# Order of the gated embedding, the output projection and the query projection in a one-core transformer block kernel

## The chip, the cores and the metric

The kernel runs on one core of one Trainium2 chip. Its time is the device time of one execution in microseconds (us); several executions give a median. One further execution was recorded by the hardware profiler; all rows below come from that one.

Engine names: PE is TensorE (matmul), with PEld for its weight loads, DVE is VectorE, ACT is ScalarE, POOL is GpSimd, SP is SyncE, which here issues most of the DMA transfers.

## The reference, cut to what matters

The block works on 256 tokens (S) of 2048 columns (D), in float32. The part around the change is:

```
merged = gate0 * (yp @ w_branch_pool) + gate1 * (ya @ w_branch_attn)
y      = merged @ w_out                      # 2048 x 2048
x      = layer_norm(ALPHA * x + y, ln1_g, ln1_b)
q      = x @ peer_wq                         # query projection, 2048 x 2048
s1, s2 = q's halves against two tables of 128 keys -> top 16 -> 16 picks and gates per head
f      = sum over picks of gelu(x @ u[id]) * gate * v[id]      # 16384 experts
e      = sigmoid(x @ ple_gate_w) * (p @ ple_w)                 # gated embedding
x      = layer_norm(ALPHA * x + f + e, ln2_g, ln2_b)
```

The kernel computes x @ u for all experts, so the tables `u` and `v` are streamed whole, as other weights are.

## The kernel before, in words

**Weights as units.** All weights are cut into units of 128 x 1024 float32 (512 KB). A unit goes through a ring: SP loads it into one of four RAW slots; ACT copies it to one of four HI slots with the high part of each number; DVE makes LO = RAW - HI in one of two slots (line 765); PE multiplies with HI and then with LO. Each product is thus three products: activations high with HI, activations low with HI, activations high with LO. In the order of each engine's program ACT's conversion (`conv`, line 453) runs three units ahead of PE (`ACT_LEAD`), DVE's one unit ahead (`DVE_LEAD`). SP may load a slot again when DVE has made LO of its last content (`lo_ready`); ACT may write HI of unit u when PE has done unit u-4; DVE may write LO of unit u when PE has done unit u-2 (`unit_done`). Everything an engine does is one queue in program order; semaphores are the only links between the engines.

**Two shapes of unit.** `w_unit` keeps weights stationary and streams activations: 8 matmuls of 128x512 (line 1350) and 8 of 128x256 (line 1356). `n_unit` keeps activations stationary and streams the weights: 8 matmuls of 128x512 with HI (line 1370) and 4 with LO (line 1377). Its results fill all eight PSUM banks: for each of two token tiles, four quarters of 512 columns (`nbank(tt, q)`); an even unit writes quarters 0 and 1, an odd one quarters 2 and 3.

**The phases in order** (units): ..., branch 32, wout 32, plew 4, wq 32, pleg 32, u 256, vtab 256. `branch` makes the two branch outputs, which DVE multiplies with their gates and adds in GT (lines 993, 994, 997). `wout` is the output projection. Its activations, the merged blocks, are staged two at a time: ACT copies the high part (line 610) when PE has done the units that read the slot, DVE makes the low part (line 1006), one block for two units. `plew` is p @ ple_w, from the same two slots.

**The first norm.** DVE adds y to ALPHA*x in eight pieces of 128x512 (line 1022) as the last wout unit of each column half is done, takes statistics (line 778), centres whole rows (line 784), waits for ACT's square root (line 475, with a load of its table), makes five small steps (lines 770 to 774), and rescales (line 790). ACT copies the plew result from PSUM to PW (line 624, eight pieces), PE then transposes x in 32 pieces into all eight banks (line 1392, `turn`), ACT takes the high part (line 481) and DVE the low part (line 812).

**After it.** `wq` runs with `w_unit`; ACT and DVE take each block of q out of PSUM (lines 641 and 848), PE multiplies it with the keys (line 1548) into bank 4, ACT takes the scores (line 632). After wq PE waits for the last scores to be taken and runs `pleg` (x @ ple_gate_w) with `n_unit` over all eight banks. ACT then applies the sigmoid in eight pieces (line 658), and the first `u` unit waits for the first four of them. In `u` DVE also does the top-k of one score set in each round of eight units. In the second half of u PE also makes one-hot products (line 1608), whose results DVE multiplies into the expert buffer (`spread`, line 1209); `vtab` is again `n_unit`, with stationary blocks that ACT (line 723) and DVE (line 1269) stage from the expert buffer.

**The end of u.** DVE's order after the last conversion is: `halves` (line 848, needs ACT's copy at line 710 of the last u result), `spread` (line 1209), `gated` (line 1202, needs ACT's gelu at line 713), then the low part of vtab's first block (line 1269).

## Time and profile before

| | us |
|---|---|
| median of 3 runs | 2329.09 (2329.08 to 2331.0) |
| the profiled execution | 2324.55 |
| its span, first to last instruction | 2322.9 |
| PE busy in the span | 2251.4 (97%) |
| DVE, ACT, POOL busy | 66%, 46%, 2% of the span |
| mean granted TensorE clock | 0.993 |

The DMA queues move 425 MB, 183 GB/s on average. In a timeline row the columns are start in us, duration in us, engine, source line, operation, output and inputs, shape and count of instructions merged in the row; in square brackets the idle time of that engine just before it and the instruction that ended the idle time. Matmuls overlap, and the end of a group of matmuls is modelled, so the last one's duration reaches past the start of the next group. PEclk in a windows row is the granted TensorE clock as a share of 2.4 GHz; 0.50 is 1.2 GHz.

### The profile page before, as it was taken

What the parts mean: (1) busy time and instruction counts of PE and PEld (TensorE: products, weight loads), DVE (VectorE), ACT (ScalarE), POOL (GpSimd) and SP (SyncE); (2) the same over time, 40 slices, a digit from 0 to 9 for tenths busy, and PEclk for the clock granted to TensorE, in tenths of its full rate; (3) what the DMA queues carried; (4) which work ended last, traced back from release to release, by engine and by line L of the source; (5) the groups of instructions that cost most, each with busy time, mean ns of one, the idle gap of its engine ahead of it and who ended that gap; (6) DMA issues with size and microseconds to landing.
All of it is one profiled execution on the core that took longest, in us unless ns stands there. A gap on an engine that the chain in (4) does not pass through costs nothing.

```text
span 2322.9 us, 39704 instructions
## 1 busy us (share of the span) xinstructions
PE 2251.4 (97%) x12176; PEld 1946.1 (84%) x12176; DVE 1534.6 (66%) x2806; ACT 1069.4 (46%) x1494; POOL 43.7 (2%) x89
## 2 busy tenths in 40 slices
PE   6999999899899999999999999999999999999996
PEld 5888888898688888888888888888888888888885
DVE  6547666665744479998888888887555555555556
ACT  3444555544444454445554444444444444444442
POOL 1000000000000000001000000000000000000000
PEclk9999999999999999999999999999999999999998
DMA  7555555455455656565555554545666666666663
GB/s 246 187 181 176 183 179 177 158 180 190 164 179 173 195 175 204 181 208 190 188 168 163 161 163 160 162 161 159 191 194 197 202 204 200 204 206 200 202 194 119
DMA packets 115714, 425.31 MB, mean 183 GB/s; under 512 B 13352, under 2 KB 13368, under 8 KB 114528
## 3 DMA queue, kind: packets, MB, share of 16 engines
q1 hardware_dynamic: 112608, 412.14, 55.8%
q0 software_dynamic: 3072, 12.72, 1.7%
q8 instruction: 20, 0.33, 0.1%
q14 instruction: 14, 0.11, 0.0%
HBM read 420.60 MB, written 6.31 MB: 184 GB/s over the span
## 4 chain that ended last, share of the span: by engine, by line
PE 87%; DVE 7%; issue 3%; DMA 2%; ACT 1%; DVEq 0%; SPq 0%; ACTq 0%
PE ps L1350 27%; PE ps L1370 25%; PE ps L1356 14%; PE ps L1377 12%; PE ps L1608 2%; DVE w_lo L765 2%; PE ps L1334 1%; PE ps L1338 1%; PE ps L1333 1%; DMA ln_gb<-in_ln_in 1%; DMA raw<-in_w_in 1%; DMA raw<-in_u 0%; DVE bn L778 0%; PE ps L1392 0%; PE ps L1478 0%
## 5 line engine op out<-in xcount | busy, mean ns | idle before, releaser
L765 DVE TENSOR_TENSOR w_lo<-raw,w_hi 128x1024 fp32r<-128x1024 f32 x774 | 946.5, 1223 | 491.1 <-PE ps L1377 420.5
L453 ACT ACTIVATE w_hi<-raw 128x1024 fp32r<-128x1024 f32 x774 | 821.2, 1061 | 972.8 <-DMA raw<-in_peer_v 375.9
L1350 PE MATMUL ps<-x_t_hi_lo,w_hi 128*128 128x512 f32 x3328 | 848.7, 397 | 4.6 <-ACT ple_gate L658 2.0
L1350 PEld LDWEIGHTS ps<-x_t_hi_lo,w_hi 128*128 128x128 f32 x3328 | 597.6, 189 | 114.6 <-issue 5.7
L1370 PE MATMUL ps<-w_hi,x_t_hi_lo 128*128 128x512 f32 x2592 | 643.4, 391 | 9.6 <-issue 3.2
L1370 PEld LDWEIGHTS ps<-w_hi,x_t_hi_lo 128*128 128x128 f32 x2592 | 488.0, 188 | 112.0 <-issue 6.5
L1356 PEld LDWEIGHTS ps<-x_t_hi_lo,w_lo 128*128 128x128 f32 x3328 | 452.8, 190 | 38.7 <-DVE w_lo L765 5.5
L1356 PE MATMUL ps<-x_t_hi_lo,w_lo 128*128 128x256 f32 x3328 | 464.7, 283 | 1.5 <-DVE w_lo L765 1.2
L1377 PE MATMUL ps<-w_lo,x_t_hi_lo 128*128 128x512 f32 x1296 | 347.4, 390 | 0.0
L1377 PEld LDWEIGHTS ps<-w_lo,x_t_hi_lo 128*128 128x128 f32 x1296 | 244.1, 188 | 50.7
L1189 DVE TENSOR_SCALAR onehots<-iota,i_t,gate_t 128x128 f32<-128x128 bf16 x256 | 77.8, 352 | 0.0
L1608 PE MATMUL ps<-onehots 128*128 128x128 f32 x512 | 77.1, 275 | 0.0
L1608 PEld LDWEIGHTS ps<-onehots 128*128 128x128 f32 x512 | 68.0, 192 | 0.0
L1185 DVE TENSOR_TENSOR onehots<-i_t,iota 128x256 f32<-128x256 bf16 x128 | 54.0, 422 | 19.0 <-DVE experts L1209 14.9
L1269 DVE TENSOR_TENSOR x_t_hi_lo<-experts,x_t_hi_lo 128x256 fp32r<-128x256 f32 x128 | 53.5, 419 | 0.1
L723 ACT ACTIVATE x_t_hi_lo<-experts 128x256 fp32r (+1 forms) x128 | 51.0, 400 | 0.1
L848 DVE TENSOR_TENSOR hidden<-ps,hidden 128x256 f32<-128x256 f32 x64 | 27.2, 425 | 29.3 <-ACT hidden L710 29.3
L848 DVE TENSOR_TENSOR gates_t<-ps,gates_t 128x256 f32 (+1 forms) x32 | 13.5, 423 | 45.8 <-ACT gates_t L513 45.8
L713 ACT ACTIVATE hidden<-hidden 128x256 f32<-128x256 f32 x64 | 26.8, 419 | 36.6 <-DVE hidden L848 36.6
L1209 DVE TENSOR_TENSOR experts<-ps,experts 128x512 f32 (+1 forms) x64 | 43.6, 681 | 0.0
L710 ACT ACTIVATE hidden<-ps 128x256 f32<-128x256 f32 x64 | 24.5, 383 | 38.0 <-PE ps L1356 35.7
L848 DVE TENSOR_TENSOR experts<-ps,experts 128x256 f32 x64 | 27.2, 425 | 16.3 <-ACT experts L668 10.1
(202 smaller groups left out, 1013.4 us busy)
## 6 DMA issues: line engine op xcount, KB each, us to landing
raw<-in_u SPq DMA_DIRECT2D x256, 512.0 KB, 4.4
raw<-in_peer_v SPq DMA_DIRECT2D x256, 512.0 KB, 4.7
raw<-in_w_in SPq DMA_DIRECT2D x128, 512.0 KB, 4.2
raw<-in_branch SPq DMA_DIRECT2D x32, 512.0 KB, 4.0
raw<-in_wout SPq DMA_DIRECT2D x32, 512.0 KB, 3.7
raw<-in_wq SPq DMA_DIRECT2D x32, 512.0 KB, 3.8
raw<-in_pleg SPq DMA_DIRECT2D x32, 512.0 KB, 3.8
x<-in_x SPq DMA_DIRECT2D x2, 1024.0 KB, 6.4
```

What stands on the lines that cost most here:

```text
L453: nc.scalar.activation(HI[:, u % 4, :], RAW[:, u % 4, :], ACT.Copy).then_inc(hi_ready, 1)
L723: nc.scalar.activation(XH[:, c % 4, :], BUF[:, bass.ds(val(i, 4, c), 1), :].rearrange("p a t -> p (a t)"), ACT.Copy).then_inc(ah_ready, 1)
L765: v.tensor_tensor(LO[:, u % 2, :], RAW[:, u % 4, :], HI[:, u % 4, :].bitcast(F32), ALU.subtract) \
L848: v.tensor_tensor(dst, PS[:, bank, S:2 * S], dst, ALU.add).then_inc(joined, 1)
L1185: ch.tag(v.tensor_tensor(OH[:, n % 2, :, 0, :], both.unsqueeze(2).to_broadcast([P, 2, P]), IOTA[:, :].unsqueeze(1).to_broadcast([P, 2, P]) ...
L1189: ins = v.tensor_scalar(OH[:, n % 2, r, 1, :], IOTA[:, :], I2T[:, bass.ds(t, 1)], GATET[:, bass.ds(t, 1)], ALU.is_equal, ALU.mult)
L1269: v.tensor_tensor(XL[:, c % 4, :], BUF[:, bass.ds(val(i, 4, c), 1), :].rearrange("p a t -> p (a t)"), XH[:, c % 4, :].bitcast(F32), ALU.su ...
L1350: mm(PS[:, bank, :], w(HI, u % 4)[:, k, :], XHL[:, 8 * half + k, :, :].rearrange("p a t -> p (a t)"), start=(half == 0 and k == 0), stop=F ...
L1356: r = mm(PS[:, bank, 0:S], w(LO, u % 2)[:, k, :], XH[:, 8 * half + k, :], start=False, stop=(half == 1 and k == 7))
L1370: mm(nbank(tt, 2 * half + q), stn[:, tt * P:(tt + 1) * P], HI[:, u % 4, q * 512:(q + 1) * 512], start=(first and s == 0), stop=False, skip ...
L1377: r = mm(nbank(tt, 2 * half + q), ah[:, tt * P:(tt + 1) * P], LO[:, u % 2, q * 512:(q + 1) * 512], start=False, stop=last, skip_group_chec ...
L1608: r = mm(PS[:, 4 + g % 2, o:o + P], OH[:, n % 2, t, 0, :], OH[:, n % 2, t, 1, :], start=True, stop=True)
```

## The change

1. The phase `plew` leaves the ring of units. Its four weight units are loaded by POOL's DMA queue into a buffer of their own (PRAW), spaced by wout units, and converted during wout into buffers of their own (PH, PL). p is split into high and low parts (YAH, YAL) early in wout.
2. The merged blocks are split into high and low parts for all 16 blocks (XH, XL) during `branch`, two blocks at the end of each round, and not staged in wout.
3. `wout` runs by column halves: 16 units for the left half, then 16 for the right. The residual adds and the statistics of the left half are done by DVE during the right half.
4. `pleg` moves from behind wq to ahead of it and also runs by column halves. The plew products run right after wout, the last part of them split by quarters. The norm is centred and rescaled by quarters of 512 columns, and PE transposes two column blocks at a time, between the units of the first half of pleg, into banks 2, 6, 3, 7. The sigmoids of the left half are done during the right half.
5. The square-root table is loaded ahead of wout. u follows wq at once; the last key scores are made after the first u unit, and each top-k round waits for its own scores.
6. At the end of u DVE does `spread`, then the low part of vtab's first block, then `halves` and `gated`; ACT takes that block's high part ahead of its last copy and gelu. PE's first vtab units wait for `joined`, not for `gated`.

```diff
-          ("plew", 2), ("wq", 16), ("pleg", 16), ("u", 128), ("vtab", 128)]
+          ("pleg", 16), ("wq", 16), ("u", 128), ("vtab", 128)]
...
+            pool.wait_ge(merged_ready, KD)
+            for j in range(4):
+                pool.wait_ge(unit_done, BASE["wout"] + 1 + 3 * j)
+                pool.dma_start(PRAW[:, j, :], a["plew"][j % 2, :, (j // 2) * UNIT:(j // 2 + 1) * UNIT]
+                               ).then_inc(plew_in, 16)
             pool.wait_ge(al_ready, KD)
             pool.wait_ge(ah_ready, KD)
             for n in range(2):
+                pool.wait_ge(unit_done, BASE["wout"] + 16 + 5 * n)
                 pool.dma_start(LNG[:, n, :], ...
...
+            def merged_hi(i):                                   # ACT
+                for c in range(2):
+                    act.wait_ge(merged_ready, i * 2 + c + 1)
+                    nc.scalar.activation(XH block 2i+c, GT block 2i+c, ACT.Copy).then_inc(ah_ready, 1)
+            run("branch", 8, 4, {3: merged_hi}, pre=sig_pre)
+            nc.scalar.preload_act_table(ACT.Sqrt)
+            for j in range(20):
+                conv(None, 4, BASE["wout"] + j + ACT_LEAD)
...
+                if j >= 16:
+                    act.wait_ge(plew_in, 64)
+                    nc.scalar.activation(PH[:, j - 16, :], PRAW[:, j - 16, :], ACT.Copy).then_inc(plew_hi, 1)
+            run("wout", 8, 4, {}, start=5)
             std_of(2)
+            ple_out(1, (0, 1))
+            conv(None, 4, pb + 3)
+            ple_out(2, (2,))
+            xt_hi(1, (0,))
+            ple_out(3, (3,))
+            for g in range(1, 8):
+                xt_hi(1, (g,))
+                conv(None, 4, pb + 2 * g + 2)
+                conv(None, 4, pb + 2 * g + 3)
...
+            for j in range(28):                                 # DVE
+                conv(None, 4, BASE["wout"] + j + DVE_LEAD)
...
+                if 16 <= j < 20:
+                    dve.wait_ge(plew_hi, j - 16 + 1)
+                    v.tensor_tensor(PL[:, j - 16, :], PRAW[:, j - 16, :], PH[:, j - 16, :], ALU.subtract)
+                if 20 <= j < 24:
+                    added(*first_cols[j - 20])
+                if j >= 24:
+                    quarter(X0, *first_cols[j - 24])
+            run("wout", 8, 4, {}, start=7)
+            dve.wait_ge(unit_done, BASE["wout"] + 32)
+            for tt, q in last_cols:
+                added(tt, q)
+            for tt in range(NT):
+                stats(X0, tt, (2, 3))
+            variance()
+            root(2)
+            centre_cols(X0, LNG, cols[0])
+            rescale_cols(X0, LNG, cols[0])
+            centre_cols(X0, LNG, cols[1])
+            xt_lo(1, (0,))
+            rescale_cols(X0, LNG, cols[1])
+            conv(None, 4, pb + 1)
+            for g in range(1, 8):
+                if g < 3:
+                    centre_cols(X0, LNG, cols[g + 1])
+                xt_lo(1, (g,))
+                conv(None, 4, pb + 2 * g)
+                if g < 3:
+                    rescale_cols(X0, LNG, cols[g + 1])
+                conv(None, 4, pb + 2 * g + 1)
...
+            for half in range(2):                               # PE
+                for k in range(KD):
+                    if half == 0:
+                        pe.wait_ge(al_ready, k + 1)
+                    n_unit(None, 4, BASE["wout"] + KD * half + k, XH[:, k, :], XL[:, k, :], ..., half)
+            pe.wait_ge(n_dve, 4)
+            plew_part(0, 0)
+            plew_part(0, 1).then_inc(plew_done, 1)
+            pe.wait_ge(n_dve, 8)
+            plew_part(1, 0, (0,))
+            plew_part(1, 1, (0,)).then_inc(plew_done, 1)
+            plew_part(1, 0, (1,))
+            pe.wait_ge(n_act, 6)
+            turn(1, (0,))
+            plew_part(1, 1, (1,)).then_inc(plew_done, 1)
+            for half in range(2):
+                for k in range(KD):
+                    if half == 0 and k % 2 == 0:
+                        pe.wait_ge(xh_ready, 8 + k // 2 + 1)
+                        pe.wait_ge(xl_ready, 8 + k // 2 + 1)
+                    n_unit(None, 4, BASE["pleg"] + KD * half + k, XH[:, k, :], XL[:, k, :], ..., half)
+                    if half == 0 and k % 2 == 0 and k < KD - 2:
...
+                        turn(1, (g,))
...
-            pe.wait_ge(joined, 80)
-            pe.wait_ge(peer_sb, 8)
-            for c in range(KD):
-                for j in range(2):
-                    n_unit(None, 4, BASE["pleg"] + 2 * c + j, XH[:, c, :], XL[:, c, :], c == 0, c == KD - 1)
...
-                        pe.wait_ge(n_act, 12 if j == 0 else 16)
...
+            a_lo(None, 0)                                       # DVE, end of u
+            halves(None, 2 * B_ITERS - 1)
             gated(None, 2 * B_ITERS - 1)
-            a_lo(None, 0)
             a_lo(None, 1)
...
-            pe.wait_ge(dve_evac, 79)
+            pe.wait_ge(joined, 80 + NK - 1)
```

## Rows read from the trace of the kernel before

**Rows 1.** The page: busy time by engine.
```profile
PE 2251.4 (97%) x12176; PEld 1946.1 (84%) x12176; DVE 1534.6 (66%) x2806; ACT 1069.4 (46%) x1494; POOL 43.7 (2%) x89
```

**Rows 2.** Waits of PE, 405 to 920 us: waiter, releaser, us, times, longest.
```profile
PE ps L1392 <- DVE x L790: 5.3, 2, 4.6
...
PE ps L1370 <- DVE x_t_hi_lo L1006: 2.0, 1, 2.0
...
PE ps L1548 <- DVE peer_q L848: 0.9, 1, 0.9
```

**Rows 3.** Windows, 30 wout units: busy PE, PEld, DVE, ACT, POOL; clock; DMA share, GB/s.
```profile
521.20:602.80 81.60, 81.60 (x361) 67.62 (x360) 43.14 (x45) 36.47 (x45) 1.06 (x2) 1.00 0.61 195
```

**Rows 4.** Timeline from branch to wout.
```profile
518.36 2.08 PE L1370 MATMUL ps<-w_hi,x_t_hi_lo 128*128 128x512 f32 x8 [2.49 <-issue]
```

**Rows 5.** Timeline from the last wout unit to the first wq unit.
```profile
604.62 1.07 PE L1377 MATMUL ps<-w_lo,x_t_hi_lo 128*128 128x512 f32 x4
604.74 4.87 DVE L1022 SCALAR_TENSOR_TENSOR x<-x,ps 128x512 f32<-128x512 f32 x8
607.27 2.11 PE L1370 MATMUL ps<-w_hi,x_t_hi_lo 128*128 128x512 f32 x8 [1.59 <-DVE x L1022]
...
614.93 2.47 DVE L778 BATCH_NORM_STATS2 bn<-x 128x6 f32<-128x512 f32 x4
...
618.94 4.61 DVE L784 SCALAR_TENSOR_TENSOR x<-x,mean_var,ln_gb 128x2048 f32<-128x2048 f32 x2
...
622.45 4.03 ACT L624 ACTIVATE p_w<-ps 128x512 f32<-128x512 f32 x8 [0.17 <-PE ps L1377]
...
624.60 0.16 DVE L770 RECIPROCAL rstd<-std 128x2 f32<-128x2 f32 x1
...
625.59 4.87 DVE L790 SCALAR_TENSOR_TENSOR x<-x,rstd,ln_gb 128x1024 f32<-128x1024 f32 x4
...
628.12 6.11 PE L1392 MATMUL ps<-ident,x 128*128 128x128 f32 x31 [0.66 <-DVE x L790]
...
631.12 4.88 DVE L812 TENSOR_TENSOR x_t_hi_lo<-ps,x_t_hi_lo 128x512 fp32r<-128x512 f32 x8 [0.66 <-ACT x_t_hi_lo L481]
...
633.99 2.09 PE L1350 MATMUL ps<-x_t_hi_lo,w_hi 128*128 128x512 f32 x8
```

**Rows 6.** Windows of 2 us in the same stretch, clock 0.56 and 0.50.
```profile
616.00:618.00 2.00, 2.00 (x7) 1.57 (x6) 1.93 (x5) 0.00 (x0) 0.00 (x0) 0.56 0.77 240
...
628.00:630.00 2.00, 1.88 (x9) 1.88 (x10) 2.00 (x3) 0.00 (x0) 0.00 (x0) 0.50 0.03 10
```

**Rows 7.** Timeline: 16 transposes at full clock.
```profile
419.04 1.91 PE L1487 MATMUL ps<-ident,att 128*128 128x128 f32 x16
```

**Rows 8.** Timeline: the end of one round of branch.
```profile
504.59 0.42 DVE L993 TENSOR_TENSOR gates_t<-ps,gates_t 128x256 f32 x1 [1.79 <-PE ps L1338]
...
505.26 1.06 ACT L453 ACTIVATE w_hi<-raw 128x1024 fp32r<-128x1024 f32 x1 [1.52 <-DMA raw<-in_branch]
...
505.92 2.57 DVE L765 TENSOR_TENSOR w_lo<-raw,w_hi 128x1024 fp32r<-128x1024 f32 x2
...
508.99 1.12 PE L1338 MATMUL ps<-ya_hi,w_lo 128*128 128x256 f32 x8
```

**Rows 9.** Tile raw, 590 to 612 us: DMA time to landing.
```profile
DMA to landing us min/median/max: 3.5/3.8/8.9
```

**Rows 10.** Timeline: wq to pleg, and pleg to u.
```profile
732.80 2.08 PE L1370 MATMUL ps<-w_hi,x_t_hi_lo 128*128 128x512 f32 x8 [0.73 <-issue]
...
822.10 2.12 PE L1350 MATMUL ps<-x_t_hi_lo,w_hi 128*128 128x512 f32 x8 [1.99 <-ACT ple_gate L658]
```

**Rows 11.** Timeline: u to vtab.
```profile
1598.09 1.23 DVE L765 TENSOR_TENSOR w_lo<-raw,w_hi 128x1024 fp32r<-128x1024 f32 x1
...
1602.65 3.66 PE L1370 MATMUL ps<-w_hi,x_t_hi_lo 128*128 128x512 f32 x8 [2.71 <-DVE x_t_hi_lo L1269]
```

**Rows 12.** The page: `spread`, the costliest groups (count, busy, mean ns, idle before).
```profile
L1209 DVE TENSOR_TENSOR experts<-ps,experts 128x512 f32 (+1 forms) x64 | 43.6, 681 | 0.0
```

266 lines of the change are left out of this document (142 added, 124 removed).

## The prediction

> **What bounds the kernel now.** I read the busy times of the page first. PE is busy for 97% of the span, DVE for 66% [rows 1], so PE bounds the kernel, and only two things can change its time: the work PE is given, and the stretches in which PE waits or runs below full clock. The change gives PE the same matmuls and transposes, so I looked for the waits. The list of PE's waits between 405 and 920 us [rows 2] shows them to be few, each standing at the border of two phases. Inside a phase there are none: 30 units of wout take 81.60 us with PE busy for 81.60 [rows 3]. That gives 81.60 / 30 = 2.72 us for an `n_unit`, of wout, plew or pleg, and says that the ring of weights keeps up there. The timelines at the borders then give the size of each gap.
>
> **A, branch to wout.** PE stands still for 2.49 us before the first wout unit [rows 4], because the first blocks are staged only when branch is over and DVE's staging stands behind the last merge. In the new order block 0 is split rounds before. What PE waits for is banks 0 and 1, taken by the merge before last, 5.8 us earlier (two branch units). Gain 2.5.
>
> The cover of this edit is the branch phase. ACT's high parts now wait for the last merge of a round, and behind them in ACT's queue stand two sigmoids and the conversion of the unit after next; behind DVE's low parts stands LO of the next unit. I follow one round from the rows [rows 8]. The merge starts at 504.59 and ends when LO starts, by 505.92. ACT's high part (of 128x256: under the 0.50 of a copy twice as large, 4.03 / 8 [rows 5]; I take 0.4) ends at 506.3, DVE's low part (0.42, as a merge operation of this shape) at 506.8, LO (2.57 / 2 = 1.28) at 508.1. PE needs this LO at 508.99. That leaves 0.9 us, so I cost the edit at nothing. ACT's conversion that ran at 505.26 ends at 506.3 + two sigmoids 0.9 + 1.06 = 508.3; it is for the unit two later, which starts some 4 us after that. If the cover is gone, every one of 8 rounds pays the excess. From below a gain in branch is excluded: PE is without gaps there.
>
> **B, wout to the first unit after the norm.** Before: the last wout matmuls end at 604.62 + 1.07 = 605.69, the first wq matmul starts at 633.99 [rows 5]. That is 28.3 us. The work in it at full clock is 4 plew units, 4 x 2.72 = 10.88, and 32 transposes at 1.91 / 16 = 0.12 each [rows 7], 3.8. So 28.3 - 14.7 = 13.6 us are waits (1.59, 2.0, 4.6 and 0.7 [rows 2, 5]) and half clock: the granted clock was 0.56 at 616 to 618 and 0.50 at 628 to 630, that is 1.2 GHz, after PE had stood still for 2 us and for 5 us [rows 6].
>
> After: I set time 0 at the end of wout's last unit. DVE has done the left half's adds and statistics in wout's second half, where a unit takes 2.72 and LO 1.23, so an added operation of 0.6 fits. DVE, on the path: four adds at 4.87 / 8 = 0.61 end at 2.7 (with 0.25 for the first hop); four statistics at 2.47 / 4 = 0.62 and two sums of 0.3 end at 5.8; variance and the root on ACT (table already loaded), 0.4, and five small steps, 1.0 (625.59 - 624.60), 7.3; centring 2 x 512 columns, 4.61 / 4 = 1.15 (4.61 is for 2 x 2048), 8.5; rescaling them, 2 x 0.61, 9.7. ACT: root at 6.1, four copies of plew at 4.03 / 8 = 0.50, one conversion of 1.06, two copies, end at 10.4. PE: 5.44 + 2.72 + 1.36 = 9.5 us of plew, then it waits for ACT until 10.5; four transposes until 11.0; the last plew part of 1.36 until 12.3. The block's high part (0.5) ends at 11.8, its low part (4.88 / 8 = 0.61) at 12.5. PE therefore waits 1.0 us and then 0.2; I allow 0.3 for hops between engines: 1.5. At least 0, at most 5: the latter if the plew copies and the norm met one behind the other and not side by side.
>
> Then pleg's first half. Two units and four transposes take 5.44 + 0.48 = 5.9 us. In the two pairs that still carry the norm DVE has to do centring 1.15, low part 0.61, rescaling 1.22 and two LO, 2.46: 5.4. Tight, but the low part that PE needs next comes early in that order, half a pair ahead, and from the third pair DVE has 3.1. I take 0.3 for the seven switches between units and transposes; bounds 0 and 4 (each of the first three pairs late by 1.3, the length of one LO). B: 13.6 - 1.5 - 0.3 = 11.8 gained.
>
> **The plew loads** move from SP's ring to POOL's queue and its four conversions (1.06 on ACT, 1.23 on DVE each) into wout units 16 to 19. There DVE has 2 x 1.23 of 2.72. No 512 KB load from POOL's queue into a weight buffer is in the trace. The nearest row: while POOL's two 1024 KB loads of the norm's weights were in flight, one ring load took 8.9 us to land instead of 3.8 [rows 9]. A conversion runs three units ahead of PE, 8.2 us less its own 1.06, so a single load may be 5 us late and PE does not see it. I take 0; bounds 0 and 3 (a load late by twice 5 us: 10.2 - 7.1). What waits behind POOL's new waits is only the norm's weights, due some 20 us later.
> The Trainium skill says (DMA: Bandwidth & Descriptors, "Queues, rings and completion order") that each DMA engine takes turns between the queues that have work. By that rule each POOL load delays a ring load by up to its own length, and the 8.9 us agrees; it speaks for the second rival, and by it the sum could be up to 3 us less.
>
> **C, pleg ahead of wq.** Before, PE waits 0.93 for the last q block, 0.73 for the last scores and 1.99 for the sigmoids [rows 2, 10], together 3.65. After, wq starts on banks whose sigmoids were done beneath the second half of pleg; the other four (0.5 each) have two wq units, 5.6 us. u follows wq with the same unit shape; the last scores are made one unit later and taken off PE's path. Gain 3.6; bounds 2 (if wq's start meets ACT's four sigmoids) and 3.65.
>
> **D, u to vtab.** Before: gap 2.71, and then 8 matmuls took 3.66 us instead of 2.1 [rows 10, 11], so 1.6 lost to half clock. After: DVE is free at 1599.3 (1598.09 + 1.23), `spread` 0.68 [rows 12] to 1600.0, high part on ACT 0.4 to 1600.5, low part 0.42 to 1600.9, PE at 1601.15 instead of 1602.65: gain 1.5. A gap of 1.2 us then is left. Gaps of 1.59, 1.99 and 2.49 were followed by matmuls at full clock [rows 4, 5, 10], so I count the 1.6 too. D: 3.1; bounds 1.5 and 4.3.
>
> **Sum.** 2.5 + 11.8 + 3.6 + 3.1 = 21.0 us. The profiled execution took 2324.55 and would take 2303.5. The median of the runs is 2329.09, 4.5 above the profiled one; I set the forecast against the median: 2329.1 - 21.0 = 2308.1.
>
> The Trainium skill says (TensorE: Matmul & The Clock Gate, "Part 4: PE-mode transpose") that transposes do not count as busy for the clock gate. Here 16 transposes behind matmuls ran in 1.91 us at full clock [rows 7], so a short run of them did no harm. By that rule the transposes set among plew and pleg units make the clock fall of the first rival likelier.
>
> **Rivals.**
> 1. *Part of the gain is given back around the first transpose.* If ACT's queue (root, copies, conversion, copies) or DVE's chain runs 1.5 us longer than added up, PE's gap grows to 2.5 us, two gaps stand close, and the clock falls as it did at 616 us. Before, the four plew units took 15.0 us (607.27 to 622.45 - 0.17 [rows 5]), 2.0 of it a wait [rows 2], instead of 10.9: the fall cost 2.1. With one such fall, 1.5 more of waiting and the first pairs of pleg late by 4: 7.6 less, 2315.7. For it: 5.4 of 5.9 us in the first pairs. Against it: the low part needed stands early in the queue. Chance 0.12.
> 2. *The loads disturb the ring.* POOL's loads and double conversions make wout wait. At the other end of the bound, if two of the six loads (four plew, two of norm weights) each push a ring load by twice 5 us, PE sees 10.2 - 7.1 = 3 each, 6 together, and one clock fall of 2.1: 2316.2. Against it: the conversion's lead. Chance 0.05.
> 3. *The split in branch makes the kernel slower.* Place: LO behind the low parts at each round's end. Price: 8 rounds x (chain - 0.9 us of margin). The loads of the ring wait for LO, so a late round also makes the next load late. It decides from 21.0 / 8 = 2.6 us per round, a chain 3.5 us longer than I added up. With 4 us: 8 x 3.1 = 24.8, so 2332.9. For it: the margin is the smallest of all. Against it: the chain has three operations of 0.4 us. Chance 0.03.
> 4. *Less of it is reached than it says*: an edge wait takes the place of another with the same length in A and C. Then B and D alone remain, 14.9: 2314.2. Against it: all waits named there are for work done many us before. Chance 0.05.
>
> **How the numbers follow.** Forecast 0.75. The likeliest value is 2308. Downward the bounds add 1.5 (B's waits at 0) + 0.3 + 1.2 (D): 2305, and the runs scatter by some us against the profiled one (4.5): 2303. Upward the range takes in rivals 1 and 4: 2316. About 0.1 is left outside on either side together. A measurement of this kernel tells 0.2%, 4.7 us, from no change. Faster than 2324.4: all but rival 3 and a remainder, 0.95; within 0.2%: 0.02; slower: 0.03.
>
> **What would show it.** In the new trace: no PE wait at branch's end (A); 15 to 18 us between wout's last matmul and pleg's first, PE at full clock throughout, one wait of about 1 us ahead of the first transposes released by ACT's plew copy, one of a few tenths by the low part (B); 81.6 us for 30 wout units as before; no wait from pleg to wq and from wq to u (C); a gap of 1.2 us ahead of vtab followed by 8 matmuls in 2.1 (D); branch rounds of 11.5 us. Wrong would be: low clock after the first transposes, ring loads landing over 9 us, PE waiting for LO in branch, or pleg's first 16 units above 47.5 us (16 x 2.72, and 28 transposes at 0.12).

## The result and the profile after

The changed kernel takes 2303.11 us (median of 4 runs, 2302.41 to 2305.83), the kernel before 2329.09 us (4 runs, 2326.51 to 2331.0). The ratio is 0.9892, interval 0.988 to 0.9904: 26 us, where 21.0 were forecast. The two profiled executions stand 18.7 us apart (2324.55 and 2305.83). Both differences have to be accounted for, and they have different reasons.

The page of the changed kernel, busy time by engine. It answers to [rows 1]: the same 12176 matmuls and transposes, busy for 4.9 us less.

```profile
PE 2246.5 (97%) x12176; PEld 1940.3 (84%) x12176; DVE 1533.7 (67%) x2816; ACT 1068.3 (46%) x1494; POOL 45.8 (2%) x93
```

Branch to wout, PE's timeline of the changed kernel (start, duration, engine, line, operation, operands, shape, count, and in brackets the idle time before it with its releaser). It answers to [rows 4]: the first wout unit now starts while branch's last matmuls drain, with no bracket at all.

```profile
517.92 1.12 PE L1410 MATMUL ps<-ya_hi,w_lo 128*128 128x256 f32 x8
518.88 1.99 PE L1440 MATMUL ps<-w_hi,x_t_hi_lo 128*128 128x512 f32 x8
```

Thirty wout units and the 32 pleg units with their 28 transposes, windows of the changed kernel (length; busy PE, PEld, DVE, ACT, POOL; clock; DMA share, GB/s). The first answers to [rows 3]: the length is again 81.60, but PE is busy for 80.63 of it. The second has PE busy for its whole length.

```profile
524.48:606.08 81.60, 80.63 (x357) 66.44 (x356) 46.50 (x44) 35.75 (x36) 2.64 (x5) 1.00 0.73 247
622.28:709.86 87.58, 87.58 (x401) 72.60 (x400) 46.83 (x46) 39.83 (x43) 0.00 (x0) 1.00 0.57 187
```

(The 81.60 is a coincidence: this window is cut ahead of a group's modelled end, and has 357 matmuls where that of [rows 3] has 361. Counted from phase start to phase end, wout took 88.33 us and before 87.33.) The 0.97 us that are missing are one new wait. The timeline of all engines at that place:

```profile
563.16 0.53 POOL L430 DMA_DIRECT2D ln_gb<-in_ln  x1 [16.08 <-PE ps L1447]
...
564.09 12.61 SPq L321 DMA_DIRECT2D raw<-in_wout  x4
...
571.78 1.06 ACT L471 ACTIVATE w_hi<-raw 128x1024 fp32r<-128x1024 f32 x1 [3.66 <-DMA raw<-in_wout]
...
572.75 1.04 ACT L636 ACTIVATE plew_hi<-plew_raw 128x1024 fp32r<-128x1024 f32 x1
...
573.82 1.22 DVE L1075 TENSOR_TENSOR plew_lo<-plew_raw,plew_hi 128x1024 fp32r<-128x1024 f32 x1 [3.31 <-ACT plew_hi L636]
574.96 1.22 DVE L797 TENSOR_TENSOR w_lo<-raw,w_hi 128x1024 fp32r<-128x1024 f32 x1
...
576.24 1.20 PE L1447 MATMUL ps<-w_lo,x_t_hi_lo 128*128 128x512 f32 x4 [0.97 <-DVE w_lo L797]
```

Read it from below. PE waited for LO of its unit (574.96). Nothing that this LO needs was late: its HI was made at 566.11. It stood in DVE's queue behind a plew low part (573.82), which had waited 3.31 us for the plew high part; that one stood in ACT's queue behind a conversion for the unit after PE's (571.78), which had waited 3.66 us for its load. The load was issued at 564.09, just behind POOL's load of the norm's weights at 563.16, and landed 7.7 us later. The ring's loads in this stretch (tile raw, 515 to 607 us), answering to [rows 9]:

```profile
DMA to landing us min/median/max: 3.8/4.9/7.7
```

Wout to pleg, PE's timeline. It answers to [rows 5]. Instead of 28.3 us from wout's last matmul to the next phase there are 12.1 (607.37 to 619.48), and the only idle time is 0.42 us.

```profile
606.30 1.07 PE L1447 MATMUL ps<-w_lo,x_t_hi_lo 128*128 128x512 f32 x4
...
617.36 0.66 PE L1470 MATMUL ps<-ident,x 128*128 128x128 f32 x4 [0.42 <-ACT p_w L644]
...
619.48 2.06 PE L1440 MATMUL ps<-w_hi,x_t_hi_lo 128*128 128x512 f32 x8
```

What releases it, from the timeline of ACT and DVE: two of ACT's copies of the plew result ahead of the transposes, DVE's low part ahead of pleg.

```profile
613.34 2.04 ACT L644 ACTIVATE p_w<-ps 128x512 f32<-128x512 f32 x4
616.20 1.10 ACT L644 ACTIVATE p_w<-ps 128x512 f32<-128x512 f32 x2
...
618.68 0.69 DVE L858 TENSOR_TENSOR x_t_hi_lo<-ps,x_t_hi_lo 128x512 fp32r<-128x512 f32 x1
```

The clock there, a 2 us window that answers to [rows 6] (0.56 and 0.50 before): full, that is 2.4 GHz.

```profile
618.00:620.00 2.00, 1.93 (x9) 1.28 (x8) 2.00 (x5) 1.16 (x3) 0.00 (x0) 1.00 0.00 0
```

Pleg to wq, wq to u with the last key scores behind the first u unit, and u to vtab: PE's timeline, answering to [rows 10, 11]. No bracket is left but the last one.

```profile
709.86 0.84 PE L1422 MATMUL ps<-x_t_hi_lo,w_hi 128*128 128x512 f32 x3
...
806.02 2.00 PE L1422 MATMUL ps<-x_t_hi_lo,w_hi 128*128 128x512 f32 x8
...
808.81 0.61 PE L1634 MATMUL ps<-keys_t,peer_q 128*128 128x128 f32 x4
...
1585.60 2.08 PE L1440 MATMUL ps<-w_hi,x_t_hi_lo 128*128 128x512 f32 x8 [1.21 <-DVE x_t_hi_lo L1340]
```

Last, a stretch that the change does not touch, hundreds of us ahead of it. This execution waited 2.39 us there and then ran at half clock (timeline of PE, and a window); the profile of before waited 0.90 us at the same place (at 215.25) and kept its clock.

```profile
216.84 1.48 PE L1525 MATMUL ps<-q_k_head 64*128 64x128 f32 x8 [2.39 <-ACT q_k_head L561]
```

```profile
218.00:220.00 2.00, 2.00 (x6) 1.47 (x5) 1.54 (x7) 0.68 (x1) 0.00 (x0) 0.50 0.71 231
```

Branch starts at 426.60 instead of 423.45, 3.15 us later. From branch's start to the end the changed kernel is 18.7 + 3.15 = 21.85 us shorter, and this is the figure that the sum of 21.0 speaks of. In the medians: 18.72, and 4.54 that the profile of before lies below its median, and 2.72 that the profile of after lies above its own, make 25.98.

### The profile page after: what moved, and what is told of

Same layout as the page of the kernel before. It is cut to its first block, busy times and chain, and to the rows that moved or that the text cites. A ratio compares the mean times of both kernels' runs of the same rounds, so it can differ in the third digit from the quotient of the medians.

```text
span 2304.2 us, 39472 instructions
## 1 busy us (share of the span) xinstructions
PE 2246.5 (97%) x12176; PEld 1940.3 (84%) x12176; DVE 1533.7 (67%) x2816; ACT 1068.3 (46%) x1494; POOL 45.8 (2%) x93
## 4 chain that ended last, share of the span: by engine, by line
PE 87%; DVE 6%; issue 3%; DMA 2%; ACT 1%; DVEq 1%; SPq 0%; ACTq 0%
PE ps L1422 27%; PE ps L1440 25%; PE ps L1428 14%; PE ps L1447 12%; PE ps L1686 2%; DVE w_lo L797 2%; PE ps L1406 1%; PE ps L1410 1%; PE ps L1405 1%; DMA ln_gb<-in_ln_in 1%; DMA raw<-in_w_in 1%; DMA raw<-in_u 0%; PE ps L1556 0%; DMA raw<-in_wout 0%; DVE bn L809 0%
## 5 line engine op out<-in xcount | busy, mean ns | idle before, releaser
L1440 PE MATMUL ps<-w_hi,x_t_hi_lo 128*128 128x512 f32 x2560 | 633.2, 389 | 1.3 <-DVE x_t_hi_lo L1340 1.2
L1440 PEld LDWEIGHTS ps<-w_hi,x_t_hi_lo 128*128 128x128 f32 x2560 | 479.8, 188 | 101.0 <-issue 1.9
L1447 PE MATMUL ps<-w_lo,x_t_hi_lo 128*128 128x512 f32 x1280 | 342.2, 389 | 1.0 <-DVE w_lo L797 1.0
```

The costliest lines, as they stand in the source:

```text
L1440: mm(nbank(tt, 2 * half + q), stn[:, tt * P:(tt + 1) * P], wh[:, q * 512:(q + 1) * 512], start=(first and s == 0), stop=False, skip_group_ ...
L1447: r = mm(nbank(tt, 2 * half + q), ah[:, tt * P:(tt + 1) * P], wl[:, q * 512:(q + 1) * 512], start=False, stop=last, skip_group_check=True)
```

## The experiments

Four theories stood: that gaps A, B, C and D of the prediction each contribute what the sum says (T1); that the gain is one of the clock, not of the gaps (T2); that the wait at 216 us belongs to the change (T3); that the 5 us between 26 and 21 are a matter of which execution was profiled (T4). Each kernel is compared with runs of the kernel before on its own chip: their median is 2330.04 us for e0 to e3, 2327.5 for e5 to e7 and 2328.31 for e8 to e11. The changed kernel run again (e0) is the reference for the undo experiments. "Above e0" is the difference of two medians; for e5, e6, e7 and e11 it is one between two chips and uncertain by the 2.5 us that these medians differ, so there the border in the trace is the evidence.

**e0: the changed kernel again**, without an edit.

> The changed kernel once more, as the common yardstick of this set. Its profile showed a gap of 2.4 us and low clock at 217 us, in a phase that the change does not touch, and the span grew by 3.2 us ahead of branch. Theory 1 (that gap is scatter between executions, set by when a load of the ring lands): another profile shows 0.9 us there or 2.4 us by chance, and from branch on the same 1878 us within 0.5. Theory 2 (the changed code costs 3 us ahead of branch): 2.4 us there again. Time 2303 us, ratio to before 0.989.

Measured: 2302.05 us (2300.93 to 2303.03, 4 runs) against 2330.04; ratio 0.9885 (0.9868 to 0.9903). PE's timeline at the place of the untouched wait:

```profile
215.38 0.93 PE L1525 MATMUL ps<-q_k_head 64*128 64x128 f32 x8 [0.84 <-ACT q_k_head L561]
```

0.84 us, as before the change: the 2.39 was one execution's, and T3 falls. Ahead of the transposes stood again 0.42 us, ahead of vtab 1.21, from wout's end to pleg again 12.11; the wait for LO in wout was 0.5. From branch's start to the end of the span this execution took 1877.5 us (2300.7 - 423.19), the first one 1877.6 (2304.2 - 426.60).

**e1, A undone: the merged blocks are staged in wout.**

```
-            run("branch", 8, 4, {3: merged_hi}, pre=sig_pre)
+            run("branch", 8, 4, {}, pre=sig_pre)
...
             for j in range(20):                     # wout; DVE likewise with merged_lo
+                if j < KD:
+                    merged_hi(j // 2, (j % 2,))
                 conv(None, 4, BASE["wout"] + j + ACT_LEAD)
```

> The merged blocks are split inside wout's first half, each ahead of its unit, and no longer in branch; all else as changed. Theory (part A): the gap between branch and wout is back, 2.3 to 2.5 us, since DVE's first low part stands behind the last merge; 2.4 us more than the changed kernel. Rival (the split in branch costs in branch what it saves at the border): the branch phase gets shorter and the total stays, 0 us.

Measured: 2309.13 us (2306.2 to 2311.91, 5 runs), ratio 0.9914 (0.9898 to 0.9929), 7.1 above e0 where 2.4 was expected. PE's timeline:

```profile
519.78 2.73 PE L1443 MATMUL ps<-w_hi,x_t_hi_lo 128*128 128x512 f32 x8 [1.96 <-DVE gates_t L1042]
```

The gap came back (1.96), but more with it. From branch's start to the end this execution took 8.8 us more than e0: 2.1 by this border, 1.5 by a fall of the clock behind it (2.73 for 8 matmuls instead of 2.09, and more in the next ones), 1.5 by another fall behind the gap ahead of branch, which the edit does not touch, and 3.5 in wout, where my edit stages blocks too late (30 units in 85.87 us against e0's 82.38; the longest waits are 0.39 at 532.95 and 1.21 at 551.12 for blocks, and 0.85 for LO at 581.64). The undo was not a clean one, and was done again:

**e11, A undone with the staging two blocks ahead.**

```
+            merged_hi(0)
             for j in range(20):                     # DVE likewise with merged_lo
+                if j < KD - 2:
+                    merged_hi(j // 2 + 1, (j % 2,))
                 conv(None, 4, BASE["wout"] + j + ACT_LEAD)
```

> As the run without the split in branch, but two blocks are split ahead of wout's first conversion and the others two blocks ahead of their unit. That earlier run showed, beside the gap of 2.0 us at the border and low clock behind it, 1.6 us of waits for later blocks that its own tight staging made. Theory (part A is the gap at the border alone): one gap of 2.3 us ahead of wout, none behind it; 2.3 us more than the changed kernel, 4 with a fall of the clock. Rival (splitting inside wout costs by itself, since wout also carries the plew conversions): waits within wout stay and the total is 5 us or more above the changed kernel.

Measured: 2304.99 us (2303.34 to 2307.99, 4 runs), ratio 0.99 (0.9884 to 0.9915), 2.9 above e0. The waits for blocks are gone; left are one gap, with full clock behind it, and a wait for LO of 0.82 at 573.76, at the place of e0's 0.5:

```profile
516.45 2.09 PE L1445 MATMUL ps<-w_hi,x_t_hi_lo 128*128 128x512 f32 x8 [1.96 <-DVE gates_t L1043]
```

From branch's start to wout's first matmul it took 94.39 us, 2.1 more than e0. So A is the gap, 2 to 2.5 us; the rest of e1 was its tight staging and two falls of the clock.

**e2, C undone: sigmoids and last scores late**, all eight pieces of the sigmoid behind pleg, and the last key scores ahead of u.

```
-                if j >= 16:
-                    act.wait_ge(unit_done, pb + 16)
-                    ple_gate((j - 16) // 2, j % 2)
...
-            for q in (2, 3):
+            for q in range(4):
...
+            key_scores(64 + 2 * HEADS, 1).then_inc(peer_scores, 1)
+            pe.wait_ge(peer_sb, HEADS)
             for j in range(8):                      # u
```

> All eight sigmoids come after pleg instead of four beneath its second half, and the last scores are made and taken ahead of the first u unit, with PE waiting; all else as changed. Theory (part C): two gaps come back, 2.0 us ahead of wq (four sigmoids of 0.5) and 0.9 + 0.7 us ahead of u; 3.6 us more. Rival (the order of the phases, not these two covers, made the gain): under 1 us more.

Measured: 2309.25 us (2307.0 to 2310.6, 5 runs), ratio 0.9913 (0.9897 to 0.9928), 7.2 above e0 where 3.6 was expected. PE's timeline:

```profile
709.50 3.35 PE L1419 MATMUL ps<-x_t_hi_lo,w_hi 128*128 128x512 f32 x8 [2.36 <-ACT ple_gate L648]
...
808.41 0.71 PE L1631 MATMUL ps<-keys_t,peer_q 128*128 128x128 f32 x4 [0.93 <-DVE peer_q L891]
810.80 2.11 PE L1419 MATMUL ps<-x_t_hi_lo,w_hi 128*128 128x512 f32 x8 [1.68 <-ACT scores L672]
```

The three gaps add to 4.97 and the fall behind the first to 1.3 (3.35 instead of 2.09): 6.3 of the 7.2. That C is a matter of these waits holds; my 3.6 had taken the gaps from the old order, where they were 1.99, 0.93 and 0.73, so that the last one, for the scores, is the one that I had too short by most.

**e3, D undone: the old end of u** (`halves`, `spread`, `gated`, then the low part), with ACT's order there as before too.

```
-            pe.wait_ge(joined, 80 + NK - 1)
+            pe.wait_ge(dve_evac, 79)
...
-            a_lo(None, 0)
-            halves(None, 2 * B_ITERS - 1)
             gated(None, 2 * B_ITERS - 1)
+            a_lo(None, 0)
             a_lo(None, 1)
```

> The order of DVE and ACT at the end of u as before, all else as changed. Theory (part D): the gap ahead of vtab is 2.7 us again instead of 1.2, and the clock falls behind it, so that the first 8 matmuls take 3.7 us instead of 2.1: 3.1 us more. Rival (the clock's fall before was chance): 1.5 us more, 8 matmuls in 2.1.

Measured: 2304.54 us (2302.88 to 2307.43, 5 runs), ratio 0.9899 (0.9883 to 0.9915), 2.5 above e0.

```profile
1583.56 2.09 PE L1439 MATMUL ps<-w_hi,x_t_hi_lo 128*128 128x512 f32 x8 [2.71 <-DVE x_t_hi_lo L1340]
```

The gap is the 2.71 us of [rows 11] to the hundredth, but the 8 matmuls took 2.09 and not 3.66. The profiled execution took 2303.81, 1.4 more than e0's (2302.38), which is what the gap alone costs; the median's 2.5 lies between that and the 3.1 with a fall. The same gap is followed by a fall of the clock in one execution and not in another. That made the kernel before the next thing to look at.

**e4: the kernel before again**, without an edit.

> The kernel before once more, for its profile. Its gaps stand at the same places with the same lengths in every execution. Theory 3 (behind a gap of about 2 us or more the clock falls in some executions and not in others, which costs 1 to 2 us each time): the fall behind the vtab gap (2.7 us) or the second plew gap (2.0 us) of the first profile may be missing, and another may stand behind the wout gap (2.5 us) or the u gap (2.0 us); the runs scatter by 5 us or more. Rival (the fall follows from the length of the gap alone): the same falls at the same places as in the first profile. Ratio 1.000.

Measured: 2327.28 us (2322.81 to 2330.64, 11 runs), ratio 1.0002 (0.9993 to 1.0011). The profiled one took 2330.64, 6.1 more than the one of the rows ahead. PE's timeline at three borders:

```profile
519.94 3.56 PE L1370 MATMUL ps<-w_hi,x_t_hi_lo 128*128 128x512 f32 x8 [2.49 <-issue]
...
613.68 2.11 PE L1370 MATMUL ps<-w_hi,x_t_hi_lo 128*128 128x512 f32 x8 [2.23 <-DVE x L1022]
...
621.48 2.90 PE L1370 MATMUL ps<-w_hi,x_t_hi_lo 128*128 128x512 f32 x8 [2.07 <-DVE x_t_hi_lo L1006]
```

The gap of 2.49 is the one of [rows 4], which had 2.08 behind it; now 3.56. The eleven runs show that part of the scatter goes with the clock: mean clock 0.993 goes with 2322.81, 2325.37 and 2326.67, clock 0.990 with 2329.19 and 2329.26. A thousandth of 2329 us is 2.3 us. But at 0.991 stand 2326.9 and 2330.64, so the clock is not all of it. The changed kernel has 0.994 to 0.996.

From branch's start to the end this execution took 1905.45 us (2329.0 - 423.55) and the one of the rows ahead 1899.45 (2322.9 - 423.45). Added up along PE's timeline, the 6.0 us are:

| stretch | us | what |
|---|---|---|
| branch | 1.5 | a fall of the clock at its start, behind a gap of 2.50 that the change leaves as it is |
| first wout unit | 1.6 | the fall behind the gap of 2.49 |
| 30 wout units | 2.6 | 84.21 instead of 81.60, at a granted clock of 1.00 |
| ahead of plew | 0.6 | a gap of 2.23 instead of 1.59 |
| plew to vtab | -0.3 | |

So half of it is low clock and half is waiting. One pair of wout units, timeline of ACT, DVE and PE:

```profile
563.91 1.06 ACT L453 ACTIVATE w_hi<-raw 128x1024 fp32r<-128x1024 f32 x1 [1.88 <-DMA raw<-in_wout]
...
565.52 0.42 DVE L1006 TENSOR_TENSOR x_t_hi_lo<-gates_t,x_t_hi_lo 128x256 fp32r<-128x256 f32 x1 [0.91 <-ACT x_t_hi_lo L610]
...
566.08 2.10 PE L1370 MATMUL ps<-w_hi,x_t_hi_lo 128*128 128x512 f32 x8
```

ACT's conversion waited for its load; behind it in ACT's queue stands the copy of the next merged block, behind that DVE's low part, and PE starts when this is made (due at 565.84). The wait is some 0.2 us, and there is one like it for many of the blocks from 552 us on. In the first profile none of ACT's conversions between 530 and 605 us was released by a load and the ring's loads took 3.7 us in the median; here 22 were, after 35.9 us of waiting together, and the median is 4.7. The changed kernel waits for loads there just as much (34.3 us in 22 conversions, 32.7 in 20 in e0), but has no merged block behind its conversions. T4 holds: the profile of before was of one of the shorter executions.

**e5, left half late: adds and statistics of the left half behind wout.**

```
-                if 20 <= j < 24:
-                    added(*first_cols[j - 20])
-                if j >= 24:
-                    quarter(X0, *first_cols[j - 24])
...
-            for tt, q in last_cols:
+            for tt, q in first_cols + last_cols:
                 added(tt, q)
```

> DVE adds the left column half to the residual and takes its statistics only after wout's last unit, with the right half's; all else as changed. Theory (the halves of wout take DVE work off the path): the first transposes start four adds and four statistics later, 8 x 0.62 = 5.0 us; PE waits 2.7 us ahead of the plew products and about 2.7 ahead of the transposes. 5.0 us more, and up to 2 x 2 us if the clock falls. Rival (plew hides it): 2.7 us more, one gap.

Measured: 2306.81 us (2305.33 to 2308.15, 5 runs), ratio 0.9915 (0.9901 to 0.9928), 4.8 above e0. From wout's last matmul to pleg 16.87 us, 4.76 more than 12.11; expected were 5.0. PE's timeline:

```profile
606.80 0.70 PE L1433 MATMUL ps<-plew_hi,ya_hi 128*128 128x512 f32 x2 [2.66 <-DVE x L1061]
...
608.06 1.06 PE L1433 MATMUL ps<-plew_hi,ya_hi 128*128 128x512 f32 x2
...
618.89 0.66 PE L1463 MATMUL ps<-ident,x 128*128 128x128 f32 x4 [0.70 <-ACT p_w L644]
```

The wait sits in two places. Behind the first one (2.66) the clock fell (1.06 for two matmuls, not 0.62), which cost nothing here: the norm's chain was the longer one, and slow matmuls only shortened the second wait.

**e6, the norm applied whole, not by quarters.**

```
-            centre_cols(X0, LNG, cols[0])
-            rescale_cols(X0, LNG, cols[0])
-            centre_cols(X0, LNG, cols[1])
+            for c in cols:
+                centre_cols(X0, LNG, c)
+            for c in cols:
+                rescale_cols(X0, LNG, c)
             xt_lo(1, (0,))
```

> DVE centres all four quarters and then rescales all four before the first low part; all else as changed. Theory (the quarters let PE start): ahead of the first low part stand 5 more operations pairs of 1.41 us, so pleg's first unit starts 7.0 us later, with gaps of about 4.6 us ahead of the transposes and 2.8 ahead of that unit. 7.0 us more, up to 11 with falls of the clock. Rival (pleg's first pairs, free of norm work, run faster and give it back): under 5 us more.

Measured: 2309.82 us (2308.12 to 2310.48, 5 runs), ratio 0.9926 (0.9912 to 0.9939), 7.8 above e0; wout to pleg 18.68, 6.57 more than 12.11, expected 7.0. PE's timeline:

```profile
618.94 0.30 PE L1466 MATMUL ps<-ident,x 128*128 128x128 f32 x1 [3.92 <-DVE x L848]
...
624.13 2.07 PE L1436 MATMUL ps<-w_hi,x_t_hi_lo 128*128 128x512 f32 x8 [1.18 <-issue]
```

Undoing the split by quarters alone thus costs 6.6 us, half of the 12.85 us that B measures below.

**e7, the norm's weights loaded later**, at wout units 22 and 26 instead of 16 and 21, when the four plew conversions are over.

```
-                pool.wait_ge(unit_done, BASE["wout"] + 16 + 5 * n)
+                pool.wait_ge(unit_done, BASE["wout"] + 22 + 4 * n)
```

> POOL's two loads of the norm's weights (1024 KB each) wait for wout units 22 and 26 instead of 16 and 21, so they no longer meet the conversions of the plew weights; all else as changed. Theory (the 1.0 us wait of PE for LO at 576 us comes from the ring load that took 7.7 us beside the first of them): no such wait, 0.5 to 1.0 us less. Rival (the doubled conversions of ACT and DVE in units 16 to 19 make it): the wait stays.

Measured: 2301.5 us (2299.52 to 2302.5, 4 runs), ratio 0.9894 (0.9879 to 0.9909). No wait for LO is left in wout, and 30 units take 81.60 us again (82.86 and 82.38 in the two profiles of the changed kernel). The late load is still there: a ring load issued at 575.73, 0.9 us behind POOL's at 574.80, took 7.8 us to land and ACT waited 5.21 us for it, but no plew parts stand in the queues any more. The time is 0.5 us below e0, the ratio 0.0009 above e0's, and the ranges overlap: that the wait went is shown, that this beats the changed kernel is not.

**e8, D alone, on the kernel before.**

```
             gated(None, 2 * B_ITERS - 1)      # now behind a_lo(None, 0) and halves(...)
...
-            pe.wait_ge(dve_evac, 79)
+            pe.wait_ge(joined, 80 + NK - 1)
```

> The kernel before with the new order at the end of u as its only edit. Theory (part D is independent of the rest): the gap ahead of vtab goes from 2.7 to 1.2 us and the clock no longer falls behind it: 3.1 us less, 2324.4. Rival (the clock's fall behind that gap is chance and counts half): 1.5 to 2.5 us less.

Measured: 2325.44 us (2322.04 to 2328.24, 11 runs) against 2328.31 (27 runs); ratio 0.9987 (0.9978 to 0.9996), 3.0 us by the ratio where 3.1 were expected; the interval runs from 0.9 to 5.1 us, so it does not tell the 3.1 from the 1.5 to 2.5 of the rival. PE's timeline at vtab, at the second plew pair, at the norm, and at the first u unit; then a window of 1 us:

```profile
1602.27 2.08 PE L1371 MATMUL ps<-w_hi,x_t_hi_lo 128*128 128x512 f32 x8 [1.21 <-DVE x_t_hi_lo L1269]
...
614.64 3.60 PE L1371 MATMUL ps<-w_hi,x_t_hi_lo 128*128 128x512 f32 x8 [2.05 <-DVE x_t_hi_lo L1006]
...
620.91 1.07 PE L1378 MATMUL ps<-w_lo,x_t_hi_lo 128*128 128x512 f32 x4
...
627.70 5.66 PE L1393 MATMUL ps<-ident,x 128*128 128x128 f32 x31 [0.66 <-DVE x L790]
...
821.57 2.50 PE L1351 MATMUL ps<-x_t_hi_lo,w_hi 128*128 128x512 f32 x8 [2.02 <-ACT ple_gate L658]
```

```profile
632.00:633.00 1.00, 1.00 (x12) 1.00 (x11) 1.00 (x2) 1.00 (x3) 0.00 (x0) 1.00 0.00 0
```

Behind the 2.02 at 821.57 the clock fell as well, which it had not done behind the 1.99 of [rows 10]. The window matters beyond D. At 632 us the clock is back at 1.00, and since 621.98 PE had done nothing but transposes (in the kernel before it came back at 633 to 634, granted 0.85, 31 transposes running since 628.12).

**e9, transposes in the gaps of the kernel before**, of the identity into a free bank, whose results nobody reads: 20 ahead of wout, 11 ahead of plew, 30 ahead of the norm's, 12 ahead of u; none ahead of vtab.

```
+            fill(6, 20)
             pe.wait_ge(dve_evac, 15)
...
+            pe.wait_ge(n_act, 1)
+            fill(0, 30)
             pe.wait_ge(n_act, 8)
             turn(1)
```

> The kernel before with transposes of the identity, whose results nobody reads, in four of its gaps: 20 between branch and wout, 11 ahead of plew, 30 while PE waits for the norm, 12 ahead of u. At 0.12 us each they fit into the gaps, so the waits end when they ended before. Theory (standing still is what makes the clock fall, and that costs the kernel before several us): full clock through wout's start, plew and the transposes of the norm, 3 to 6 us less. Rival by the page of the skill (transposes don't count as work for the clock): clock and time as before, or the fillers at half clock make the waits longer. The vtab gap is left as it was.

Measured: 2325.99 us (2323.12 to 2328.1, 11 runs), ratio 0.9986 (0.9977 to 0.9995), 2.3 below before's 2328.31 where 3 to 6 were expected. PE's timeline, and two windows:

```profile
515.97 2.34 PE L1536 MATMUL ps<-ident 128*128 128x128 f32 x20
...
622.74 3.49 PE L1536 MATMUL ps<-ident 128*128 128x128 f32 x30 [0.69 <-ACT p_w L624]
...
629.37 6.42 PE L1392 MATMUL ps<-ident,x 128*128 128x128 f32 x31 [0.73 <-DVE x L790]
...
1604.07 3.33 PE L1370 MATMUL ps<-w_hi,x_t_hi_lo 128*128 128x512 f32 x8 [2.71 <-DVE x_t_hi_lo L1269]
```

```profile
626.00:628.00 2.00, 0.23 (x3) 0.00 (x0) 1.82 (x6) 0.12 (x1) 0.00 (x0) 1.00 0.36 111
...
630.00:632.00 2.00, 2.00 (x12) 2.00 (x11) 1.70 (x2) 0.27 (x1) 0.00 (x0) 0.50 0.00 0
```

The borders that were filled up kept their clock, the unfilled one (vtab) fell. At the norm the clock was still 1.00 at 626 to 628, where before had 0.74 to 0.50, and fell when the 2.02 us between the fillers and the first real transpose had passed; the real transposes ran at 0.50 until 635 us. That took part of the gain. The plew units also started 1.0 us later behind wout than before: ACT's last conversion ahead of p's copy had waited 2.40 us for its load (604.24), and DVE's adds stand behind that copy's low part.

**e10, matmuls in the same gaps**, and 20 of one-hots ahead of vtab (not in the lines below); the same places and counts, with a matmul in place of the transpose. The lines show the edit against e9.

```
             def fill(bank, n):
                 for _ in range(n):
-                    nc.tensor.transpose(PS[:, bank, 0:P], IDENT[:, :], IDENT[:, :])
+                    mm(PS[:, bank, 0:P], IDENT[:, :], IDENT[:, :], start=True, stop=True)
```

> As the run with transposes, but with plain matmuls of the identity with itself (128x128) in the four gaps, and 20 matmuls of one-hots in the gap ahead of vtab. Theory (standing still lets the clock fall): full clock behind all five gaps, 4 to 7 us less than before. If the clock looks at the kind of work too, this run is faster than the one with transposes by more than the 1.6 us of the vtab gap. Rival (the scatter of the kernel before has another cause): same time as before, same falls.

Measured: 2329.27 us (2327.26 to 2331.8, 11 runs), ratio 1.0003 (0.9994 to 1.0012). PE's timeline:

```profile
515.67 4.62 PE L1536 MATMUL ps<-ident 128*128 128x128 f32 x40
520.06 2.09 PE L1370 MATMUL ps<-w_hi,x_t_hi_lo 128*128 128x512 f32 x8
...
625.03 6.96 PE L1536 MATMUL ps<-ident 128*128 128x128 f32 x60 [0.85 <-ACT p_w L624]
631.83 3.91 PE L1392 MATMUL ps<-ident,x 128*128 128x128 f32 x32
```

Each of these float32 matmuls shows as two records (x40 for 20 in the program) and takes twice a transpose's time, so the fillers were longer than the gaps: by 1.8 us ahead of wout (520.06, where 515.81 + 2.49 = 518.3 was due), by 0.7, 1.3 and 1.5 at plew, u and vtab, together 5.3. At the norm the border took 13.2 us instead of 11.7, 1.5 more, although the 32 transposes ran at full clock (3.91 us instead of 6.1). The second plew gap was shorter by 0.65 (1.40). In exchange every filled border kept its clock. The kernel paid 6.2 us and became 1.0 slower by the medians: the falls at those borders other than the norm's cost the kernel before some 5 us, an estimate that the interval (-1.4 to +2.8 around the 1.0) blurs by two. The 4 to 7 us expected did not come: the fillers took them. T2 falls with this: full clock at these borders is worth some 5 us and not 26, and of the 21.85 us between the two profiles at most 6 are low clock (2.1 at plew, 2.3 in the transposes, 1.65 at vtab). T1 holds: the undo runs bring the waits of A, B and C back, each at its place, and e3 that of D.

## Why the prediction was right

The forecast was 2308.0 with 2303.0 to 2316.0, the median 2303.11. The mechanism was right, border by border; that the range held was luck, by 0.1 us, and e0's median of 2302.05 lies outside it. Its lower end does not follow from its own terms either: 2305 less the 4.5 us of scatter is 2300.5, not 2303. Step by step, in the two profiles:

| step | predicted | measured |
|---|---|---|
| A, branch to wout | 2.5 | 2.47 |
| wout with the plew and norm loads | 0 (0 to -3) | -1.0, and -0.5 in e0 |
| B, wout to the unit after the norm | 11.8 | 12.85 |
| C, pleg ahead of wq | 3.6 | 4.46 |
| D, gap and clock at vtab | 1.5 + 1.6 | 1.42 + 1.65 |
| sum from branch to the end | 21.0 | 21.85 |

**A** held. The wait is gone, branch's rounds are unchanged, and the short chain of low and high parts at a round's end never reached PE: the third rival, the one that would have made the kernel slower, did not occur. e11 shows that undoing it brings back one gap of 1.96, 2.1 us at the border and 2.9 in the median.

**B.** 28.3 us became 12.11 and, in pleg, 90.38 - 32 x 2.72 = 3.34 for 28 transposes, 15.45 together. The forecast had 16.5. Two terms of the sum were mis-sized, both upward: ahead of the first transposes I had 1.0 and found 0.42 (ACT's copies ended at 617.30, 9.9 us after wout and not 10.4), and for hops, the low part and the switches between units and transposes 0.3 + 0.2 + 0.3, where 3.34 / 28 = 0.119 us per transpose leaves nothing for a switch. The first rival (1.5 us more of waiting, and a fall) did not occur. e5 and e6 show which edits carry B: undoing the early left half costs 4.8 us at this border, undoing the quarters 6.6, each within half a us of what was expected.

**The loads.** The second rival did, in small. One load took 7.7 us, 3.9 more than the 3.8 of [rows 9] and 2.8 more than its own stretch's median, and PE saw 0.97 of it; the term was set at 0 with a bound of 3. The step that failed is "a single load may be 5 us late and PE does not see it". It counts on ACT's lead of three units. But between units 16 and 19 DVE, which is only one unit ahead of PE, waits for plew high parts that stand in ACT's queue behind the conversion of the unit three ahead, and so for the load of that unit; the LO that PE needs stands behind. e7 takes the two apart: the late load comes when the plew parts are done, ACT waits 5.21 us for it, and PE does not wait.

The Trainium skill says (DMA: Bandwidth & Descriptors, "Queues, rings and completion order") that a DMA engine serves in turn the queues that have work for it. The 7.7 us behind a load of POOL's agrees, and so do the 7.8 us in e7, where the late ring load moved along with POOL's; no run here separates this from a limit on bytes per us.

**C** held, and e2 shows its waits coming back at their places. 0.8 us more came than the three gaps hold (wq and pleg took 188.11 us together, and take 183.20, with 0.45 of key scores moved into u). It lies in the ends at the gaps: the 32 units of wq took 96.43 us up to the wait for the last q block and take 96.16 now, those of pleg 87.31 and 87.04, and the last key scores 0.71 by themselves and 0.45 between two u units. A bracket is thus some 0.3 us shorter than what the gap costs; that next to a gap no group of matmuls overlaps the next one fits this, but was not tested. The 4.46 lies above the bound of 3.65, which knew only the brackets. **The fourth rival**, an edge wait that takes the place of another, did not occur: at the borders shown above no bracket stands between 619.48 and 1585.60.

**D** held with both halves in the two profiles; e8 by itself (3.0 for 3.1) agrees, but with an interval from 0.9 to 5.1. Its second half was luck. I took the fall of the clock behind the 2.71 us gap to be what this gap does; e4 and e9 have the fall too, e3 has the gap without it.

**Where it was off** is the step from the profiled execution to the median: "the median of the runs is 2329.09, 4.5 above the profiled one; I set the forecast against the median". I moved the base but let the gain stay at 21.0, as if both kernels scattered alike. They don't. From branch's start to the end the kernel before took 1899.45 and 1905.45 us (e4), the changed one 1877.6 and 1877.5 (e0): 21.85 us apart in the first pair, 28 in the second, and the 26 of the medians lies between.

The 6 us by which the kernel before scatters here are of two kinds, about equal in e4 (3.1 and 3.2 us). The first are falls of the clock, which come by chance behind gaps of some 2 us and more. The kernel before has six borders with gaps of 1.6 to 4.6 us, the changed one is left with 0.4 and 1.2 in this stretch, and the mean clock rises from 0.990 to 0.993 up to 0.994 to 0.996. The second are waits in wout, where merged blocks stand behind conversions that wait for loads. The sum has no term for them, since in the profile of before the 30 units took 81.60 us with PE busy throughout; in e4, e8 and e10, which have the same wout, they took 84.21, 82.53 and 83.26, in e9 81.60. By splitting the blocks in branch the change removes these too, which the prediction had not counted. How the 4.5 us between the profile of before and its median divide is open: e10's estimate of 5 us of falls leaves 1.5 beyond the 3.7 that the profile of before already held at plew and vtab, and the wout units lost 1.0 us more than in that profile, as a mean of the five.

The Trainium skill says (TensorE: Matmul & The Clock Gate, "Part 4: PE-mode transpose") that a transpose does not count as busy for the clock gate in the way a matmul does, and by that rule the transposes among plew and pleg units made a fall likelier. The trace does not agree: full clock from 606 to 710 us in the changed kernel, transposes and all, and in e8 a clock that came back during nothing but transposes.

## What to carry to other kernels

Where one engine is busy for 97% of the time, the gaps at the borders of phases are most of the reserve; each can be priced to within about 1 us by adding up the chain that ends it from rows of one profile (A was met within 0.1 us, B and C within 1.1 and 0.9). Work that depends on nothing in flight (a small product, a projection of other inputs) is best placed where a chain of vector work has to be waited for, and that chain is best cut so that its first quarter releases the matmuls. A lead of several units on one engine covers a late load only as long as no engine with a shorter lead waits for anything that stands behind that conversion; a small side product put between the conversions makes just this link, in the old wout as in the new one. For the median, take several profiles of the kernel before: which gaps were followed by low clock, and how late the loads ran, differs from one execution to the next, and the expected gain holds a share of each.

## What the runs showed of the hardware

The granted clock fell to 0.50 (1.2 GHz) behind gaps of the same length in one execution and not in another:

| gap, us | a fall behind it | none |
|---|---|---|
| 1.16 to 1.21 | - | the changed kernel, e0, e8 |
| 1.59 | - | [rows 5], e8 |
| 1.96 | e1 | e11 |
| 1.99 to 2.02 | e8 (ahead of u) | [rows 10], e4 |
| 2.05 to 2.07 | [rows 6], e4, e8 | e9 |
| 2.09 to 2.29 | - | e4 (2.23); ahead of branch in e0, e5, e10 |
| 2.36 to 2.39 | e2, the changed kernel (at 216 us) | - |
| 2.49 to 2.50 | e4; ahead of branch in e1, e2, e4, e6, e9 | [rows 4], e8; ahead of branch in both first profiles, e3, e7, e8, e11 |
| 2.66 | e5 | - |
| 2.71 | [rows 11], e4, e9 | e3 |
| 3.92 to 4.6 | [rows 5], e4, e6, e8 | - |

A fall cost 0.4 to 1.6 us in the first 8 matmuls behind it (2.50, 2.73, 3.56, 3.60 and 3.66 instead of 2.1), and more in the next ones where the first 8 were not long. Transposes of the identity held the clock at 1.00 where nothing else ran (e9), and it came back while nothing but transposes ran (632 us of e8). A 512 KB load of the ring that was issued 0.9 us behind a 1024 KB load of POOL's took 7.7 us to land (7.8 in e7), where the median of its stretch was 4.9. A plain float32 matmul of 128x128 is recorded twice and takes 0.23 us (4.62 / 20), a transpose of the same shape 0.12 (2.34 / 20).
